# Differential attention: query-key scores as products over the whole array

## The reference

```
q = partial_rope(q.reshape(bsz, seq, DIFF_HEADS, 2, DIFF_DH), cos, sin) * (DIFF_DH ** -0.5)
k = partial_rope(k.reshape(bsz, seq, DIFF_HEADS, 2, DIFF_DH), cos, sin)
...
def attend(q_blk):
    s = jnp.einsum('nbhqd,nbhkd->nbhqk', q_blk, k).astype(f32)
    p = jax.nn.softmax(s, axis=-1)
    a = p[0] - lam * p[1]
    return jnp.einsum('bhqk,bhkd->bhqd', a.astype(v.dtype), v)
```

## Time and profile before

| what | value |
|---|---|
| median of 3 runs | 3031.86 us (3028.08 to 3033.28) |
| the profiled execution, its own time | 3032.38 us |
| its span, first to last instruction | 3030.6 us |
| PE busy | 2956.6 us (98%) |
| DVE, ACT, POOL busy | 1725.2, 1422.1, 421.0 us |
| mean granted TensorE clock | 0.998 of full |
| the attention stage, layer 0 and layer 1 | about 512 to 792 us and 1400 to 1681 us |

### The profile page before, as it was taken

How to read it: one execution, slowest core, us unless ns; L and a number is a source line. 1 busy time by engine, 2 the same in 40 slices (tenths; PEclk the granted TensorE clock), 3 DMA queues, 4 the chain that set the end, 5 groups by cost and what they waited for, 6 DMA issues and landing times. The chain is left out here.

```text
span 3030.6 us, 51648 instructions
## 1 busy us (share of the span) xinstructions
PE 2956.6 (98%) x20584; PEld 2380.7 (79%) x20584; DVE 1725.2 (57%) x2616; ACT 1422.1 (47%) x2795; POOL 421.0 (14%) x282
## 2 busy tenths in 40 slices
PE   9999989999999999999999999999999999999999
PEld 6788778777787878778777877778888877788887
DVE  7766742677537677733767445554444455554444
ACT  4555532566424555533666345663232356632322
POOL 1554510000013445400000020000000100000000
PEclk9999999999999999999999999999999999999999
DMA  4121112221222112112121222213222221122222
GB/s 151 64 85 58 50 64 85 73 75 60 84 88 99 64 64 85 43 67 91 61 74 60 106 87 88 77 50 112 97 97 97 84 88 71 42 103 94 95 97 84
DMA packets 42688, 243.17 MB, mean 80 GB/s; under 512 B 6832, under 2 KB 7792, under 8 KB 17136
## 3 DMA queue, kind: packets, MB, share of 16 engines
q1 hardware_dynamic: 42480, 240.30, 22.6%
HBM read 233.36 MB, written 2.20 MB: 78 GB/s over the span
## 5 line engine op out<-in xcount | busy, mean ns | idle before, releaser
L320 PE MATMUL bank<-hT,ws 128*128 128x512 f32 x2112 | 872.1, 413 | 8.3 <-ACT rq L3061 2.5
L324 PE MATMUL bank<-hT,ws 128*128 128x512 f32 x2112 | 826.5, 391 | 0.0
L323 PE MATMUL bank<-hT,ws 128*128 128x512 f32 x2112 | 824.3, 390 | 0.0
L277 DVE TENSOR_TENSOR ws<-raw,ws 128x2048 fp32r<-128x2048 f32 x160 | 372.7, 2330 | 176.6 <-ACT ws L271 173.5
L271 ACT ACTIVATE ws<-raw 128x2048 fp32r<-128x2048 f32 x172 | 328.9, 1912 | 306.1 <-PE bank L320 190.1
L320 PEld LDWEIGHTS bank<-hT,ws 128*128 128x128 f32 x2112 | 397.3, 188 | 91.4 <-issue 13.0
L324 PEld LDWEIGHTS bank<-hT,ws 128*128 128x128 f32 x2112 | 396.5, 188 | 87.3
L323 PEld LDWEIGHTS bank<-hT,ws 128*128 128x128 f32 x2112 | 398.1, 188 | 67.9 <-issue 1.4
L1129 PE MATMUL bank<-uS,ws 128*128 128x512 f32 x512 | 199.2, 389 | 0.0
L1132 PE MATMUL bank<-uS,ws 128*128 128x512 f32 x512 | 199.2, 389 | 0.0
L1133 PE MATMUL bank<-uS,ws 128*128 128x512 f32 x512 | 199.2, 389 | 0.0
(11 more groups left out here) (382 smaller groups left out, 4858.6 us busy)
## 6 DMA issues: line engine op xcount, KB each, us to landing
raw<-in_w_ff SPq DMA_DIRECT2D x64, 1024.0 KB, 4.7
raw<-in_w_delta SPq DMA_DIRECT2D x32, 1024.0 KB, 4.7
raw<-in_w_diff SPq DMA_DIRECT2D x32, 1024.0 KB, 4.7
raw<-in_w_att SPq DMA_DIRECT2D x20, 1024.0 KB, 4.7
raw<-in_w_merge_a SPq DMA_DIRECT2D x16, 1024.0 KB, 4.7
raw<-in_w_merge_b SPq DMA_DIRECT2D x16, 1024.0 KB, 4.7
raw<-in_w_out SPq DMA_DIRECT2D x16, 1024.0 KB, 4.8
rows<-sum_rows SPq DMA_DIRECT2D x16, 512.0 KB, 5.7
```

What stands on the lines that cost most here:

```text
L277: dve.tensor_tensor(self.k.ws[:, c % 2, 1], self.k.raw[:, c % 2], self.k.ws[:, c % 2, 0].bitcast(F32), ALU.subtract).then_inc(self.low_don ...
L320: first = pe.matmul(out, hi, x[:, 0, k], start=(begin and k == steps[0]), stop=False)
L323: pe.matmul(out, hi, x[:, 1, k], start=False, stop=False)
L324: last = pe.matmul(out, lo, x[:, 0, k], start=False, stop=(end and k == steps[-1]))
```

## The change

It makes the scores with matmuls over all 128 rows of the array. The stationary operand of a map holds the query's high part on one half of the partitions and its low part on the other. The moving operand holds the key's high part on both halves, and in a second matmul the key's low part on both halves. Two matmuls a map give all four terms (low x low too), 4 in a unit instead of 6.

The parts are first made on the partitions where query and key lie: the high part by one ScalarE copy for each map, on 64 partitions, the low part by one VectorE subtraction for each map. Six transfers a head then bring the missing halves over: two with the query's low part (`place_query`), two with the key's high part and two with its low part (`place_key`), each of 64 partitions x 2 KB. TensorE waits for them ahead of a head's first scores. The first head's order is changed at the start of the stage, where also `st.low(1, 0)` moves from VectorE to GpSimd. The rotation's buffer is now free after `mix`.

```diff
@@ tiles
-        qk = k.sb(ctx, "qk", [P, 2, 2, 2, SEQ], F32R)
+        ql = k.sb(ctx, "q_low", [P, SEQ], F32R)
+        QS = k.sb(ctx, "q_high_and_low", [P, 2, 2, SEQ], F32R)
+        KH = k.sb(ctx, "k_high_twice", [P, 2, 2, SEQ], F32R)
+        KL = k.sb(ctx, "k_low_twice", [P, 2, 2, SEQ], F32R)
+        MAPS = (slice(0, 64), slice(64, P))
@@ gpsimd
                 pool.memset(rot[:, :, :], 0.0).then_inc(cleared, 1)
+                st.low(pool, 1, 0)
@@ sync
-                        sp.wait_ge(qk_ready, nth(h - 1, 2, j))
+                        sp.wait_ge(qk_mixed, nth(h - 1, 2, j))
...
+                def place_query(h):
+
+                    sp.wait_ge(qk_ready, nth(h, 2, 0))
+                    for m in range(2):
+                        sp.dma_start(QS[MAPS[1 - m], h % 2, m].bitcast(F32), ql[MAPS[m]].bitcast(F32)).then_inc(placed[0], 16)
+
+                def place_key(h):
+
+                    sp.wait_ge(qk_high, nth(h, 2, 1))
+                    for m in range(2):
+                        sp.dma_start(KH[MAPS[1 - m], h % 2, m].bitcast(F32), KH[MAPS[m], h % 2, m].bitcast(F32)).then_inc(placed[1], 16)
+                    sp.wait_ge(qk_ready, nth(h, 2, 1))
+                    for m in range(2):
+                        sp.dma_start(KL[MAPS[1 - m], h % 2, m].bitcast(F32), KL[MAPS[m], h % 2, m].bitcast(F32)).then_inc(placed[1], 16)
...
                 swap(0, 1)
+                place_query(0)
+                place_key(0)
                 refill(1, 0)
                 for h in range(1, HEADS):
                     swap(h, 0)
                     refill(h, 1)
                     swap(h, 1)
+                    place_query(h)
+                    place_key(h)
@@ tensor
                     if n == 0:
                         pe.wait_ge(qk_ready, nth(h, 2, 1))
+                        pe.wait_ge(placed[0], 32 * (h + 1))
+                        pe.wait_ge(placed[1], 64 * (h + 1))
                     if u > 0:
                         pe.wait_ge(p_ready, 2 * u)
-                    for t, (a, b) in enumerate(((0, 0), (0, 1), (1, 0))):
-                        for m in range(2):
-                            hp = slice(64 * m, 64 * (m + 1))
-                            last = pe.matmul(B[SB + m][:, :], qk[hp, h % 2, 0, a, n * P:(n + 1) * P], qk[hp, h % 2, 1, b],
-                                             start=(t == 0), stop=(t == 2))
-                            if t == 2:
-                                last.then_inc(s_ready, 1)
+                    for m in range(2):
+                        q = QS[:, h % 2, m, n * P:(n + 1) * P]
+                        pe.matmul(B[SB + m][:, :], q, KH[:, h % 2, m], start=True, stop=False)
+                        pe.matmul(B[SB + m][:, :], q, KL[:, h % 2, m], start=False, stop=True).then_inc(s_ready, 1)
@@ tensor, start
                 some(fill, 3 * KT + 4)
+                turn_v(0)
+                some(fill, 5)
                 scores(0)
-                some(fill, KT - 4)
-                turn_v(0)
-                some(fill, KT)
+                some(fill, KT - 1)
@@ scalar
-                    act.activation(qk[:, h % 2, j, 0], rq[:, j], ACT.Copy).then_inc(qk_high, 1)
+                    for m, hp in enumerate(MAPS):
+                        ins = act.activation((QS, KH)[j][hp, h % 2, m], rq[hp, j], ACT.Copy)
+                    ins.then_inc(qk_high, 1)
@@ scalar, start
                 st.high(act, 1, 0)
+                qk_high_part(0, 0)
                 raw_copy(0, 2)
-                qk_high_part(0, 0)
                 qk_high_part(0, 1)
+                v_turned(0)
+                z_gate(0)
                 exps(0)
-                z_gate(0)
-                v_turned(0)
@@ vector
-                    dve.tensor_tensor(qk[:, h % 2, j, 1], rq[:, j], qk[:, h % 2, j, 0].bitcast(F32), ALU.subtract).then_inc(qk_ready, 1)
+                    if j == 0 and h > 0:
+                        dve.wait_ge(placed[0], 32 * h)
+                    for m, hp in enumerate(MAPS):
+                        low = KL[hp, h % 2, m] if j else ql[hp]
+                        ins = dve.tensor_tensor(low, rq[hp, j], (QS, KH)[j][hp, h % 2, m].bitcast(F32), ALU.subtract)
+                    ins.then_inc(qk_ready, 1)
@@ vector, start
                 mix(0, 0)
+                qk_low_part(0, 0)
                 mix(0, 1)
-                qk_low_part(0, 0)
                 qk_low_part(0, 1)
-                st.low(dve, 1, 0)
@@ program
-    nc = _bacc.Bacc("TRN2", target_bir_lowering=False, num_devices=1)
+    nc = _bacc.Bacc("TRN2", target_bir_lowering=False, num_devices=1, dynamic_dma_scratch_size=2048)
```

More of the change, by code:

```diff
@@ L2245, in diff_phase @@
         "max_ready", "exp_ready", "weights_ready", "weights_turned", "weights_t_ready", "o_ready")
-    osq, orms, on_ready, yt_ready, yhi, ylo, step, astep, cleared, qk_mixed, qk_high, turned = k.sems(
+    osq, orms, on_ready, yt_ready, yhi, ylo, step, astep, cleared, qk_mixed, qk_high, turned, *placed = k.sems(
         "o_square", "o_rms", "o_normed", "y_t_ready", "y_high_done", "y_low_done", "diff_step", "diff_act_step",
-        "rotation_cleared", "qk_mixed", "qk_high_done", "angles_ready")
+        "rotation_cleared", "qk_mixed", "qk_high_done", "angles_ready", "query_placed", "key_placed")
     B, ps = k.bank, k.ps
```

## The result

The changed kernel took 3063.65 us (median of 6 runs, 3060.65 to 3072.63) where the kernel before took 3031.49 beside it (6 runs, 3028.08 to 3035.2). The ratio is 1.011, with a 95% interval of 1.0095 to 1.0125: 32.2 us slower. The forecast was 3053.0, in a range of 3037 to 3065. So the sign and the kind were right, and the size was short by a third: +21.2 was summed, +32.2 came. That it still lies in the range, 1.4 us under its end, is luck: the end was set by a rival (B) that did not come.

The account below looks back on a forecast made before the run. TensorE, busy 98% of the span, was taken to bound the kernel. Terms -4.8 + 16.8 + 3.7 + 6.4 - 0.9 = +21.2 us on the 3031.9 us median gave 3053 us, range 3037 to 3065.

Parts of the forecast that it names:

- B: Rival, score products: gaps around them belong to semaphore waits and stay, +7 us instead of -4.8, giving 3065; chance 0.05.
- products: Score products of 64 units: four full-row products replace six in three paired slots, gaining 0.075 us each, -4.8 us.
- end of the stage: Last units: first map's scores ready 0.44 us earlier where TensorE waits for weights, 0.45 a layer, -0.9 us.
- start of the stage: First scores wait for the longer chain, VectorE operations stretched beside GpSimd by 2.0 in all: +6.4 us, bounds +2.4 and +10.4.
- 1.21 us from product to turn: One unit before the change: time from last stream product to weight turn, set against 1.135 us for five full steps.
- Heads 2 to 7: First scores of twelve heads wait 1.4 us each for the key's low part to be made and transferred: +16.8 us.
- Head 1: First scores of head 1 wait 1.85 us in each layer, its period being only 7.85 us: +3.7 us.
- the same chain: At head 1, the key's low part was taken to arrive through the same steps as in heads 2 to 7.
- The other four transfers cost nothing: Query's low and key's high part transfers: made early enough to be covered by the key's low part, 0 us.
- A: Rival, heads' first scores: copies stay hidden under 2.6 us of cover, so not slower, 3029 to 3033; chance 0.11.
- C: Rival, transfers to the other half: landing takes 3.2 us rather than 2.2, 14 more, 3067; chance 0.08 with a longer start.
- a longer start: Case at the start of the attention stage: it takes longer than forecast; chance 0.08 together with C.

Follow-up runs that it names:

- number 5: The changed kernel with VectorE's subtractions for the key's low part ahead of the unit's weights instead of behind them; 3038.36 us, ratio 1.0023.
- number 6: number 5 plus a reordered start: weight chunk on VectorE before the key's mix, query's low part behind it, first scores one stream step later; 3027.47 us, ratio 0.9989.
- number 7: number 6 with VectorE writing the query's low part straight into the other half of the partitions, its two transfers removed; 3024.66 us, ratio 0.9975.
- number 1: The kernel before with four score products on all rows, no copies or transfers, sums wrong; 3023.01 us, ratio 0.9975.
- Experiment 4: The changed kernel with the start's weight chunk subtracted by VectorE again instead of GpSimd; 3059.23 us, ratio 1.0093 (4 runs).
- (3): The changed kernel with the key's last two transfers reading its high part, so not waiting for VectorE; 3043.59 us, ratio 1.0044.
- number 2: The kernel before with each high and low part made in two instructions on 64 partitions, no transfers; 3035.79 us, ratio 1.0019.

## Why the prediction was right or wrong

The differences from the kernel before, put in order, split the 32.2 us: with the head waits gone (5) +6.6, with the start's order (6) -4.3, with the query's transfers gone (7) -8.0. So the heads are 25.6, the start's order and its clock 10.9, the issues at the start 3.7, and the products, measured apart, -8.8; what is left over is 0.8.

| term | forecast | measured |
|---|---|---|
| products, and end of the stage | -4.8 - 0.9 | -8.8 (1; 8 in its profile) |
| heads' waits | +16.8 + 3.7 | +25.6 (5 against the change) |
| start of the stage | +6.4 | +14.6 (5 against 7) |
| left over | | +0.8 |
| sum | +21.2 | +32.2 |

**Products: right in kind, and the gain too small by 3 us.** The slots, the gaps and their end with the 64-row mode came as argued. What failed was "1.21 us from product to turn": the step stopped at the first turn, whose own 0.06 us more stood in the same row. With that the rows give 1.21 + 0.06 - 1.135 = 0.135 a unit, which is what was measured.

**End of the stage: did not come.** From the last unit's first scores to the first product behind the stage's last long gap it is 17.07 us in the kernel before, 17.07 in number 1 and 17.09 in the changed kernel. The -0.9 was not there; earlier scores of one map were worth nothing at the end.

**Heads 2 to 7: right.** Exponentials later by one copy, low part in two instructions, two issues, landing of 2.2 (measured 2.3), wait of 1.4 (measured 1.49). Number 5 took all of it away by moving that one subtraction. Not in the sum was the restart: behind a wait the first product is 0.47 long and the next starts 0.3 after it, not 0.23, about 1 us over twelve heads.

**Head 1: mechanism right, size off.** The step that failed is "the same chain", with "VectorE's extra subtraction of the query ends about when its next maxima may start". With a period of 7.85 instead of 8.30 it ends later than that, and the maxima and exponentials shift by 0.75 (561.57). The term was 1.85; it measured 2.77, +1.8 over two layers.

**The heads' total** is 20.5 forecast, and 12 x 1.49 + 2 x (2.79 - 0.29) = 22.9 by the waits that number 5 removed, 23.8 with the restarts. The profiles show the rest of the 25.6: from the first to the last unit the changed kernel takes 12.7 and 13.2 us more than number 5, 25.9 together. A head's first unit is 1.65 us longer and not 1.49, the unit behind it some 0.07, and 0.8 is the longer stretch at half clock in layer 1.

**The start: this step failed.** The bounds were +2.4 and +10.4, and +14.6 came. Two things were in it. First, the wait: 3.4 us was forecast (1.4 and 2.0 of stretch), 4.6 came. VectorE's two subtractions beside GpSimd's chunk lost 3.5 us (4.84 against 1.38), where 2.0 was taken "since not all four lie inside". The nearest row showed one operation stretched by 1.0, but beside GpSimd operations of 1.35 us, and not one of 5: the sum took 1.0 for the most that one operation can lose, and here a single one lost 3.4. The waits by themselves, 2 x (4.6 - 0.25) = 8.7, still lie inside the bounds. Second, the clock, which the sum did not have at all, and which took the start past them.

What the clock costs has two readings. Where it stands at half, products start 0.43 us apart and not 0.23, so that half of the time is lost: 1.7 us in layer 0 of the changed kernel and 2.5 in layer 1, where TensorE worked for 4.9 of the 6.8 us; 1.7 in each layer of number 5, from which the 14.6 was taken. So the profiles give 8.7 + 3.4 = 12.1. But a profile is one execution. The mean granted clocks of all runs, 0.9967 in number 5 and 0.9986 in number 7, give about 10 and 4 us lost in an execution (an estimate, good to 1 or 2 us): 8.7 + 6 = 14.7. Between 3 and 6 of the 14.6 us is the clock. Experiment 4 shows the stretch apart; no run changed the clock alone.

**"The other four transfers cost nothing": right** for the changed kernel, in the heads (3) and at the start too, where the key's low part is done at 533.56 and issued at 533.58. It stops being right once the chain is cut: in number 6 the query's two issues stand before the key's, and taking them out gave 3.7 us (7), of which the score products' waits for the key's low part show 3.2 (3.8 us in number 6, 0.6 in number 7). So this cost is no part of the 32.2; it was hidden under the longer chain.

**Rivals.** A falls: half-partition operations took 0.64 and 0.69, and the chain grew by more than the cover of 2.6. B falls by number 1, C by the landing of 2.3. B was also priced in two ways: +7 us, by keeping two of the three gaps, and yet called what the row groups alone leave, "a fourth slot with nothing back", which the same prediction has at +14.5. What came, a longer start, had a share of 0.08 together with C, and no bound for the clock.

## What to carry to other kernels

Before a product is saved, price what it is made of: six matmuls in three paired slots cost only 0.13 us a unit more than four full ones, and only with the gaps around the 64-row mode counted. New operands are cheap if they are early; here the loss was one subtraction that stood behind the weights on VectorE, and moving it ahead of them gave back 25.6 of 32.2 us. When a copy between partitions is needed, ask first whether the instruction that makes the data can write it there: for one part it was free, and for all of them it overfilled VectorE's queue.

## What the runs showed of the hardware

- A VectorE subtraction pair of 64x512 took 4.84 us beside a GpSimd operation of 4.61 (in both layers), and 1.38 without. The first of the pair took 4.14, until 0.5 us after GpSimd's end: here a long GpSimd instruction held a short VectorE one for as long as the two overlapped.
- 64x512 instructions cost as much as 128x512 ones: 0.64 us against 0.63 on ScalarE, 0.69 against 0.69 on VectorE. A VectorE output on the other half of the partitions cost no more (686 ns).
- A switch to 64-row products and back costs 0.30 us in gaps around three pairs (1.21 - 4 x 0.227), and 0.06 more in the first turns behind.
- Behind a wait the first 128x512 product lasted 0.47 us and the next started 0.30 after it, where 0.39 and 0.23 are usual.
- TensorE's granted clock stood at half, 1.2 GHz, for 3.4 us or twice that, at all six waits of 4.5 to 4.6 us at the start of a stage, in the profiles of three kernels. It fell between 2.2 us before the end of the wait and 0.7 us behind it. It also fell at both waits of 2.2 us in number 2's profile, but not at those of 2.3 us (number 4), 1.4 or 0.3. In other places it fell one to four times in an execution, once (736.2 us, number 4) 1.0 us behind a head's wait of 1.85 us. What decides it stays open.
